# Two transformer blocks on one core: the first weight slot in halves, norms turned by a diagonal, unread passes in PE's waits, one slot of the SSD loop moved

## Chip, cores and metric

The kernel runs on one core of a Trainium2 chip. The metric is the device time of one execution in microseconds, the median of the runs shown. Everything is computed in float32 accuracy; products with weights are made of three rounded products (fp32r), as told below.

## The reference, cut to what matters

```python
# x: 256 tokens x 1024; all weights float32
# first block
h = rmsnorm(x, norm_mix_pre); proj = h @ w_in            # then three mixers, gates, branches
x = x + rmsnorm(mixed @ w_out, norm_mix_post)            # norm 1, "use 0"
h = rmsnorm(x, norm_ffn_pre)                             # norm 2, turn 1
x = x + rmsnorm((silu(h @ gate) * (h @ up)) @ down, norm_ffn_post)   # norm 3, "use 1"
# second block
h = rmsnorm_2(x, norm1_g)                                # norm 4, turn 2
# HGRN2, mLSTM and Mamba-2 SSD mixers; the SSD ends with
yz = (y_ssd + mb_d * xs) * silu(z); y_mb = rmsnorm_2(yz in 4 groups, mb_norm_g)
x = x + mixed @ w_out
u = causal_dwconv(rmsnorm_2(x, norm2_g) @ w_up, ...)     # norm 5, turn 3
x = x + (silu(u_g) * u_v) @ w_down
return rmsnorm_2(x, final_g)                             # norm 6, no turn
def rmsnorm(x, g): return x * rsqrt(mean(x * x) + EPS) * g
```

The norm in front of the first projection is norm 0, turn 0.

## The kernel before, in words

**Layout.** The residual X holds 256 tokens as two halves h of 128 partitions with 1024 channels in two chunks c of 512. Projections want channels on partitions, so each normed input is turned: X is scaled by 1/rms, transposed on PE in 16 blocks of 128x128 and multiplied by the gain while it is read out of PSUM into XH (rounded, ACT) and XL (the rest, DVE).

**The weight stream.** 170 slots of 128x2048 words (1 MB) are loaded by SP in order into a ring of three (`raw`). For each, ACT makes `whi` (rounded, line 274, `split_hi`) and DVE `wlo` (the rest, line 281, `split_lo`), and PE does 48 products of 256 columns (line 286: XH with whi, XL with whi, XH with wlo). SP loads slot p into the place of p - 3 once `lo_ready` of that is there. `Stream.go(1)` on PE is one such slot; on ACT and DVE it is the split of slot p + 2 and then the evacuation of slot p - 1. The order of `go` and the other work on each engine is written out by hand. The first pair behind each turn (`first_pair`, line 300) takes its products in the order in which XH and XL become ready.

**The norms.** `norm_act` squares the four chunks on ACT (line 576), with the sums in a column, and takes the root (line 583); `norm_bias` (589) and the reciprocal (594) are DVE's. `scale_dve` (625) then multiplies X by the reciprocal, 512 columns at a time, and `turn_pe` (651) transposes with the identity. `post_dve` (603, 610) multiplies the output of `w_out` or `down` by its gain and adds it, scaled, to X. `add_dve` (617) only adds. ACT needs the table that has the root; `load_sqrt` (667) runs a small root at a chosen place, so that the table is loaded there. In norm 3 this stands behind the first square; for norm 6 there is none, and the load comes with the first root.

**The start.** SP issues X in two halves, the identity, the columns of gains (PC), three slots and the small tables. DVE waits for the identity and for PC ahead of its first norm. PE waits for the identity ahead of `turn_pe`.

**The SSD stage.** `ssd_pe`, `ssd_act` and `ssd_dve` go over 16 heads. For each head PE spreads a row over the partitions (1213) and does one slot; ACT makes relu and exp of it (1421, 1424) and one `go`; DVE multiplies (1459) and does one `go`. Each second head's product is added up (1383, 1466). Behind the loop DVE gates the result with z (1470), ACT squares it (1428), PE sums the squares over channels (1389), and the next slot follows.

**The tail.** Behind the last `down` slot, DVE adds four chunks (617) and scales and gains each in one operation (1913); SP stores four chunks (261).

Of the kernel before, what the change touches and what calls it, by code (L numbers as in the profile page):

```python
# [29 lines left out]
F32 = mybir.dt.float32  # L30
# [7 lines left out]
D = 1024  # L38
# [134 lines left out]
def program(nc, ctx, stream, xt, cols, consts, masks, g1w, g2w, poolw, rows_w, rows, gains, out):  # L173
# [61 lines left out]
    def _(sp):  # L235
# [23 lines left out]
        for n, (h, c) in enumerate(CHUNKS):  # L259
            sp.wait_ge(S("result_ready"), n + 1)  # L260
            sp.dma_start(out[:, h, c * 512:c * 512 + 512], scaled(h, c)).then_inc(S("result_stored"), 16)
# [43 lines left out]
    def pair_matmuls(pe, p, slot, form, rewrite=None):  # L305

        pe.wait_ge(lo_ready, p + 1)
# [231 lines left out]
    def acc(h, c):  # L539

        return bank(3 + h - 2 * c)
# [22 lines left out]
    def norm_act(act, n, use=None, loaded=False, updated=None):  # L564

        order = CHUNKS if use is None else (ORDER_OUT if use in (0, 2) else ORDER_DOWN)
        for i, (h, c) in enumerate(order):
# [10 lines left out]
            if i == 0 and use in (1, 3):  # L578
                load_sqrt(act)
# [15 lines left out]

    def post_dve(dve, n, use):

        gain = words(POST_GAIN[n], 0, D)
        dve.wait_ge(S("gain_loaded"), 16 * (n // 2 + 1))
        written = {}  # L600
        for i, (h, c) in enumerate(ORDER_OUT if use in (0, 2) else ORDER_DOWN):
            dve.wait_ge(S("norm_partial"), 4 * n + i + 1)
            written[h, c] = mark(dve, dve.tensor_tensor(scaled(h, c), acc(h, c), gain[:, c * 512:c * 512 + 512], ALU.mult))
            if c == 0:
                norm_bias(dve, n, h, i)
                continue
            norm_scale(dve, n, h)
            settled(dve, written[h, 1])
            for k in range(2):
                dve.scalar_tensor_tensor(chunk(h, k), scaled(h, k), stat(n, 8 + h), chunk(h, k), ALU.mult, ALU.add)\  # L610
                   .then_inc(S("x_updated"), 1)

    def add_dve(dve, use):

        for i, (h, c) in enumerate(CHUNKS):
            wait_acc(dve, use, (ORDER_OUT if use in (0, 2) else ORDER_DOWN).index((h, c)))
            dve.tensor_tensor(chunk(h, c), chunk(h, c), acc(h, c), ALU.add).then_inc(S("x_updated"), 1)

    def scale_dve(dve, n):

        for h in range(2):
            norm_bias(dve, n, h, 2 * h)
            norm_scale(dve, n, h)
            for c in range(2):
                dve.tensor_scalar(scaled(h, c), chunk(h, c), stat(n, 8 + h), None, ALU.mult).then_inc(S("x_scaled"), 1)
# [726 lines left out]
    def ssd_pe(pe, st):  # L1352
# [16 lines left out]
        for h in range(17):  # L1369
            if h < 16:  # L1370
# [3 lines left out]
                st.go(1)  # L1374
            if h and h % 2 == 0:
# [9 lines left out]
                i.then_inc(S("mb_o"), 1)  # L1385
        for t in range(8):
# [10 lines left out]
    def ssd_act(act, st):  # L1397
# [16 lines left out]
        for h in range(16):  # L1414
# [10 lines left out]
            st.go(1)  # L1425
# [14 lines left out]
    def ssd_dve(dve, st):  # L1440
# [10 lines left out]
        for h in range(17):  # L1451
            if h < 16:
# [8 lines left out]
                st.go(1)  # L1461
# [261 lines left out]
    def _(act):  # L1723
# [4 lines left out]
        split_hi(act, 0, 0, 0)  # L1728
# [79 lines left out]
        norm_act(act, 5, updated=8)  # L1808
# [4 lines left out]
        norm_act(act, 6, updated=12)  # L1813

    @block.vector
    def _(dve):
# [7 lines left out]
        dve.wait_ge(S("consts_loaded"), 16)  # L1824
        dve.wait_ge(S("cols_loaded"), 16)
        for h in range(2):
            dve.wait_ge(S(f"x_loaded{h}"), 16)
        scale_dve(dve, 0)
        split_lo(dve, 0, 0)
# [71 lines left out]
        add_dve(dve, 2)  # L1901
        scale_dve(dve, 5)
# [3 lines left out]
        add_dve(dve, 3)  # L1906
        dve.wait_ge(S("gain_loaded"), 48)
        gain = words(POST_GAIN[6], 0, D)
        for h in range(2):
            norm_bias(dve, 6, h, 2 * h)  # L1910
            norm_scale(dve, 6, h)
            for c in range(2):
                dve.scalar_tensor_tensor(scaled(h, c), chunk(h, c), stat(6, 8 + h), gain[:, c * 512:c * 512 + 512], ALU.mult, ALU.mult)\
                   .then_inc(S("result_ready"), 1)
# [118 lines left out]
```

## Time and profile before

| | |
|---|---|
| median of 3 runs | 1173.26 us (1172.8 to 1174.63) |
| the profiled execution | 1174.35 us, span 1172.6 us |
| busy: PE / DVE / ACT | 94% / 64% / 52% of the span |
| mean granted clock of PE | 0.977 |
| weights and inputs read | 182.17 MB, 156 GB/s over the span |

PE is matmuls, PEld its weight loads beside them, DVE, ACT and SP the other engines. Times in the rows are microseconds from the span's start. A row of the timeline has start, duration, engine, line, operation, what it writes and reads, how many were merged, and in square brackets the idle time of the engine before it and what ended it. The granted clock is a share of full speed.

### The profile page before, as it was taken

To read this page: it belongs to the slowest core of one execution; us is meant where nothing else is said; L and a number is where in the kernel's file an instruction comes from. 1 tells how busy PE (TensorE), PEld (TensorE's weight loads), DVE (VectorE), ACT (ScalarE), POOL (GpSimd) and SP (SyncE) were. 2 spreads that over 40 slices of the span, in tenths; PEclk is the share of its full clock that TensorE was granted. 3 is DMA by queue.
4 is the path that set the end of the run, shared out by engine and by line. 5 is a ranking of instruction groups with operands and counts; after the bars stand their busy time and mean duration, and the time that the engine had idled before them with its cause. 6 is when DMAs were issued, how large, how long until landed. Compare 5 with 4: busy or idle time off the path is not lost. (4 is left out here: it accounts for less than half of the span.)

```text
span 1172.6 us, 22496 instructions
## 1 busy us (share of the span) xinstructions
PE 1106.7 (94%) x9384; PEld 1048.6 (89%) x9384; DVE 753.7 (64%) x980; ACT 606.0 (52%) x784; POOL 0.2 (0%) x4
## 2 busy tenths in 40 slices
PE   6999999989999998999897899899998998999997
PEld 5999999978999997899897899889997988999996
DVE  6355566677555555688687535964646767777775
ACT  5464546345444345578564534646454446554554
POOL 0000000000000000000000000000000000000000
PEclk9999999999999998999898899999999999999999
DMA  7433434454555542344333323343443454555540
GB/s 288 177 109 110 180 144 149 176 207 162 183 185 195 190 179 108 144 157 168 109 144 110 108 108 144 144 144 134 155 176 112 181 188 155 189 204 179 179 179 37
DMA packets 26967, 184.39 MB, mean 157 GB/s; under 512 B 3064, under 2 KB 3592, under 8 KB 5128
## 3 DMA queue, kind: packets, MB, share of 16 engines
q1 hardware_dynamic: 26312, 181.38, 42.7%
q10 hardware_dynamic: 576, 1.85, 0.5%
q8 instruction: 63, 1.03, 0.3%
q14 instruction: 16, 0.13, 0.0%
HBM read 182.17 MB, written 1.05 MB: 156 GB/s over the span
## 5 line engine op out<-in xcount | busy, mean ns | idle before, releaser
L281 DVE TENSOR_TENSOR wlo<-raw,whi 128x2048 fp32r<-128x2048 f32 x170 | 388.7, 2290 | 226.9 <-ACT whi L274 222.6
L286 PE MATMUL pp<-XH,whi 128*128 128x256 f32 x1696 | 486.4, 287 | 5.7 <-DVE P L404 3.2
L286 PE MATMUL pp<-XL,whi 128*128 128x256 f32 x1696 | 481.6, 284 | 0.0
L286 PE MATMUL pp<-XH,wlo 128*128 128x256 f32 x1696 | 481.4, 284 | 0.0
L274 ACT ACTIVATE whi<-raw 128x2048 fp32r<-128x2048 f32 x170 | 323.7, 1910 | 60.3 <-PE pp L286 42.5
L286 PEld LDWEIGHTS pp<-XH,whi 128*128 128x128 f32 x1696 | 327.1, 193 | 11.7 <-DVE P L404 3.8
L286 PEld LDWEIGHTS pp<-XL,whi 128*128 128x128 f32 x1696 | 327.2, 193 | 0.8
L286 PEld LDWEIGHTS pp<-XH,wlo 128*128 128x128 f32 x1696 | 327.0, 193 | 0.0
L286 PE MATMUL pp<-Y,whi 128*128 128x256 f32 x480 | 87.2, 283 | 0.4 <-DVE HF L419 0.2
L1588 ACT ACTIVATE Y<-P 128x256 fp32r<-128x256 f32 x44 | 18.4, 418 | 132.7 <-DVE P L1621 132.7
L286 PEld LDWEIGHTS pp<-Y,whi 128*128 128x128 f32 x480 | 75.1, 192 | 0.9 <-DVE HF L419 0.4
L1534 PE MATMUL pm<-whi,Y 128*128 128x512 f32 x176 | 68.8, 391 | 0.2 <-DVE Y L1611 0.2
L1535 PE MATMUL pm<-wlo,Y 128*128 128x512 f32 x176 | 68.7, 390 | 0.0
L1536 PE MATMUL pm<-whi,Y 128*128 128x512 f32 x176 | 68.5, 389 | 0.0
L286 PE MATMUL pp<-Y,wlo 128*128 128x256 f32 x240 | 67.9, 283 | 0.0
L286 PE MATMUL pp<-whi,XH 128*128 128x256 f32 x192 | 55.3, 288 | 0.0
L286 PE MATMUL pp<-wlo,XH 128*128 128x256 f32 x192 | 54.3, 283 | 0.0
L286 PE MATMUL pp<-whi,XL 128*128 128x256 f32 x192 | 54.3, 283 | 0.0
L1605 DVE SCALAR_TENSOR_TENSOR P<-pp,PC,P 128x255 f32<-128x255 f32 (+1 forms) x88 | 36.4, 476 | 25.4 <-ACT P L1579 25.4
L286 PEld LDWEIGHTS pp<-Y,wlo 128*128 128x128 f32 x240 | 46.0, 192 | 0.0
L1536 PEld LDWEIGHTS pm<-whi,Y 128*128 128x128 f32 x176 | 33.0, 188 | 7.0
L1534 PEld LDWEIGHTS pm<-whi,Y 128*128 128x128 f32 x176 | 33.1, 188 | 6.9 <-DVE Y L1611 0.6
(296 smaller groups left out, 1291.9 us busy)
## 6 DMA issues: line engine op xcount, KB each, us to landing
raw<-stream SPq DMA_DIRECT2D x170, 1024.0 KB, 4.8
P<-gains ACTq DMA_DIRECT2D x3, 512.0 KB, 3.3
X<-xt SPq DMA_DIRECT2D x2, 512.0 KB, 4.6
out<-P SPq DMA_DIRECT2D x4, 256.0 KB, 2.0
C<-consts SPq DMA_DIRECT2D x1, 345.5 KB, 11.5
P<-rows_w ACTq DMA_DIRECT2D x1, 272.0 KB, 2.8
U<-poolw SPq DMA_DIRECT2D x1, 256.0 KB, 10.4
PC<-cols SPq DMA_DIRECT2D x1, 177.0 KB, 5.3
```

Source lines behind the costliest of these rows:

```text
L274: act.activation(whi[:, slot, :], raw[:, slot, :], ACT.Copy).then_inc(hi_ready, 1)
L281: dve.tensor_tensor(wlo[:, slot, :], raw[:, slot, :], whi[:, slot, :].bitcast(F32), ALU.subtract).then_inc(lo_ready, 1)
L286: done = pe.matmul(dst, a, b, start=first and n == 0, stop=last and n == 2, **kw)
L1534: pe.matmul(dst, Y[:, y, t], whi[:, slot, at:at + 512], start=first, stop=False, skip_group_check=True)
L1535: pe.matmul(dst, Y[:, y, t], wlo[:, slot, at:at + 512], start=False, stop=False, skip_group_check=True)
L1536: return pe.matmul(dst, Y[:, 4 + y, t], whi[:, slot, at:at + 512], start=False, stop=last, skip_group_check=True)
L1588: act.activation(Y[:, par, :], pr, ACT.Copy).then_inc(S("hidden_hi"), 1)
L1605: i = dve.scalar_tensor_tensor(c[:, lag:], src[:, 0:256 - lag], fcol("ffn_conv_w", g + (44 * k + off)), c[:, lag:], ALU.mult, ALU.add)
```

## The change

- **First slot in halves.** Slot 0 is loaded as two halves, the first ahead of the columns PC. `first_hi` and `first_lo` split each half as it comes; DVE's wait for PC moves behind them.
- **Diagonal.** `diagonal_scale` multiplies the 128x128 identity by 1/rms, and PE multiplies X, as it stands, with this diagonal (a plain f32 product) in place of the transposes.
- **Unread passes.** `turn_pe` first runs 18, 27, 27 or 8 matmuls into bank 0, which nothing reads, then waits for the scale.
- **Norms.** `load_sqrt` stands at the head of norms 3 and 6; DVE's order in `post_dve` is new for use 1; norm 5 takes its squares in the order in which the chunks are finished.
- **Last norm.** The gain is multiplied before the root, the scale after it, half of it on ACT; stores wait for their own chunk.
- **SSD.** The slot (and ACT's and DVE's `go`) of head 0 is left out and stands behind the loop: on PE ahead of the sums of squares, on ACT ahead of the squares, on DVE behind the gate.

```diff
         sp.dma_start(C[:, 0:CLEVEL], consts[:, 0:CLEVEL]).then_inc(S("consts_loaded"), 16)
+        sp.dma_start(raw[:, 0, 0:PW // 2], stream[0, :, 0:PW // 2]).then_inc(S("first_arrived"), 16)
         sp.dma_start(PC[:, :], cols).then_inc(S("cols_loaded"), 16)
-        for p in range(RING):
+        sp.dma_start(raw[:, 0, PW // 2:], stream[0, :, PW // 2:]).then_inc(arrived[0], 16)
+        for p in range(1, RING):
             load(p, p)
...
+    def first_hi(act):
+        act.wait_ge(S("first_arrived"), 16)
+        act.activation(whi[:, 0, 0:PW // 2], raw[:, 0, 0:PW // 2], ACT.Copy).then_inc(S("first_hi_ready"), 1)
+        act.wait_ge(arrived[0], 16)
+        act.activation(whi[:, 0, PW // 2:], raw[:, 0, PW // 2:], ACT.Copy).then_inc(hi_ready, 1)
+    def first_lo(dve):
+        for ready, done, at in ((S("first_hi_ready"), S("first_lo_ready"), slice(0, PW // 2)), (hi_ready, lo_ready, slice(PW // 2, PW))):
+            dve.wait_ge(ready, 1)
+            dve.tensor_tensor(wlo[:, 0, at], raw[:, 0, at], whi[:, 0, at].bitcast(F32), ALU.subtract).then_inc(done, 1)
...
+                if rewrite == 0 and need == "x_hi" and k % 4 == 0:
+                    pe.wait_ge(lo_ready if k else S("first_lo_ready"), 1)
...
+        if n in (3, 6):
+            load_sqrt(act)
         for i, (h, c) in enumerate(order):
...
-            if i == 0 and use in (1, 3):
-                load_sqrt(act)
...
+            first = [post_gain(dve, n, use, 0, 0)]
+            norm_bias(dve, n, 0, 0)
+            first.append(post_gain(dve, n, use, 0, 1))
+            norm_scale(dve, n, 0)
+            post_add(dve, n, 0, first)
+            norm_bias(dve, n, 1, 2)
+            second = [post_gain(dve, n, use, 1, 0), post_gain(dve, n, use, 1, 1)]
+        norm_scale(dve, n, 1)
+        post_add(dve, n, 1, second)
...
+    def diagonal_scale(dve, n, h):
+        norm_scale(dve, n, h)
+        dve.tensor_scalar(scale_of(h), ident, stat(n, 8 + h), None, ALU.mult).then_inc(S("x_scaled"), 1)
...
+    def idle_passes(pe, tile, width, n):
+        for _ in range(n):
+            pe.matmul(bank(0)[:, 0:width], tile[:, 0:128], tile[:, 0:width], start=True, stop=True)
+    IDLE_PASSES = {0: (RF, 384, 18), 1: (CR, 256, 27), 2: (CR, 256, 27), 3: (CR, 256, 8)}
     def turn_pe(pe, r):
+        if r == 0:
+            pe.wait_ge(S("scalars_set"), 5)
+        elif r == 1:
+            pe.wait_ge(S("masks_rounded"), 2)
+        idle_passes(pe, *IDLE_PASSES[r])
         for h in range(2):
+            pe.wait_ge(S("x_scaled"), 2 * r + h + 1)
             for j in range(KT):
-                if j % 4 == 0:
-                    pe.wait_ge(S("x_scaled"), 4 * r + 2 * h + j // 4 + 1)
-                i = pe.transpose(turned(j)[:, h * 128:h * 128 + 128], scaled(h, j // 4)[:, (j % 4) * 128:(j % 4) * 128 + 128], ident)
+                i = pe.matmul(turned(j)[:, h * 128:h * 128 + 128], X[:, h, j * 128:j * 128 + 128], scale_of(h), start=True, stop=True)
...
                 spread_row(pe, bank(h % 2), h, True).then_inc(S("mb_decay"), 1)
-                st.go(1)
+                st.go(1 if h else 0)
...
+        st.go(1)
         for t in range(8):
             if t % 4 == 0:
                 pe.wait_ge(S("mb_squares"), t // 4 + 1)
...
             act.activation(e, e, ACT.Exp, scale=-1.0).then_inc(S("mb_exp"), 1)
-            st.go(1)
+            st.go(1 if h else 0)
+        st.go(1)
         for b in range(2):
             act.wait_ge(S("mb_u"), b + 1)
...
             dve.tensor_tensor(x, x, P[:, XZ + 4 * b:XZ + 4 * b + 4, :], ALU.mult).then_inc(S("mb_u"), 1)
+        st.go(1)
         dve.wait_ge(S("mb_rms"), 1)
...
-        norm_act(act, 5, updated=8)
+        norm_act(act, 5, updated=8, order=ORDER_OUT)
...
         norm_act(act, 6, updated=12)
+        last_scale_act(act, 0, 1)
+        last_scale_act(act, 1, 1)
...
-        add_dve(dve, 2)
-        scale_dve(dve, 5)
+        add_dve(dve, 2, 0, 0)
+        add_dve(dve, 2, 1, 0)
+        norm_bias(dve, 5, 0, 0)
+        norm_bias(dve, 5, 1, 1)
+        add_dve(dve, 2, 0, 1)
+        add_dve(dve, 2, 1, 1)
+        diagonal_scale(dve, 5, 0)
+        diagonal_scale(dve, 5, 1)
...
+        add_dve(dve, 3, 0, 0)
+        last_gain(dve, 0, 0)
+        add_dve(dve, 3, 0, 1)
+        norm_bias(dve, 6, 0, 0)
+        last_gain(dve, 0, 1)
+        add_dve(dve, 3, 1, 0)
+        dve.wait_ge(S("norm_rms"), 13)
+        dve.reciprocal(stat(6, 8), stat(6, 6)).then_inc(S("last_scales"), 1)
+        dve.wait_ge(S("last_scales"), 1)
+        last_scale_dve(dve, 0, 0)
+        add_dve(dve, 3, 1, 1)
+        norm_bias(dve, 6, 1, 2)
+        last_gain(dve, 1, 0)
+        last_gain(dve, 1, 1)
+        dve.wait_ge(S("norm_rms"), 14)
+        dve.reciprocal(stat(6, 9), stat(6, 7)).then_inc(S("last_scales"), 1)
+        dve.wait_ge(S("last_scales"), 2)
+        last_scale_dve(dve, 1, 0)
```

## Rows read from the trace of the kernel before

**Rows 1.** The page's busy times, share of the span and instructions.
```profile
PE 1106.7 (94%) x9384; PEld 1048.6 (89%) x9384; DVE 753.7 (64%) x980; ACT 606.0 (52%) x784; POOL 0.2 (0%) x4
```
**Rows 2.** Timeline around turns 1, 2 and 3.
```profile
266.22 3.63 PE L651 MATMUL pm<-C,P 128*128 128x128 f32 x16 [4.19 <-DVE P L625]
275.86 0.39 PE L286 MATMUL pp<-XH,whi 128*128 128x256 f32 x1 [0.23 <-DVE wlo L281]
454.61 1.28 ACT L667 ACT_TABLE_LOAD   x1
462.54 0.88 DVE L625 TENSOR_SCALAR P<-X,SC 128x512 f32<-128x512 f32 x2
463.08 3.68 PE L651 MATMUL pm<-C,P 128*128 128x128 f32 x16 [5.12 <-DVE P L625]
973.42 1.10 PE L651 MATMUL pm<-C,P 128*128 128x128 f32 x8 [1.95 <-DVE P L625]
```
**Rows 3.** Busy times by window; the last three columns are clock, DMA, GB/s.
```profile
466.50:467.50 1.00, 1.00 (x7) 1.00 (x6) 1.00 (x3) 1.00 (x4) 0.00 (x0) 0.50 0.00 0
972.00:974.00 2.00, 0.58 (x5) 0.59 (x6) 1.36 (x6) 1.61 (x6) 0.00 (x0) 1.00 0.00 0
```
**Rows 4.** Timeline of the start, and the identity's time from issue to landing.
```profile
1.66 0.42 SPq L242 DMA_DIRECT2D C<-consts  x1
...
C<-consts SPq DMA_DIRECT2D x1, 64.0 KB, 5.1
...
7.55 0.15 DVE L589 TENSOR_SCALAR SC<-SC 128x1 f32<-128x1 f32 x1 [4.17 <-DMA PC<-cols]
11.77 3.01 ACT L660 ACTIVATE XH<-pm,PC 128x256 fp32r<-128x256 f32 x8
14.24 0.58 PE L300 MATMUL pp<-XH,whi 128*128 128x256 f32 x1 [1.63 <-DVE wlo L281]
16.32 0.41 PE L300 MATMUL pp<-XH,wlo 128*128 128x256 f32 x1
16.54 0.41 PE L300 MATMUL pp<-XH,whi 128*128 128x256 f32 x1
19.42 2.08 PE L300 MATMUL pp<-XL,whi 128*128 128x256 f32 x16
21.34 0.28 PE L286 MATMUL pp<-XH,whi 128*128 128x256 f32 x1
```
**Rows 5.** Timeline of the SSD loop's first head and of its end.
```profile
793.13 0.73 ACT L1421 ACTIVATE P<-pm,SC 128x256 f32<-128x256 f32 x2 [0.53 <-PE pm L1213]
794.33 1.90 ACT L274 ACTIVATE whi<-raw 128x2048 fp32r<-128x2048 f32 x1
898.82 2.19 ACT L1428 ACTIVATE P<-P 128x1024 f32<-128x1024 f32 x2 [5.46 <-DVE P L1470]
899.93 5.30 PE L1389 MATMUL pm<-P,C 128*4 128x256 f32 x16 [3.15 <-ACT P L1428]
```
**Rows 6.** Timeline of the tail, and the stores' time from issue to landing.
```profile
1162.61 0.69 DVE L617 TENSOR_TENSOR X<-X,pm 128x512 f32<-128x512 f32 x1 [0.67 <-PE pm L1536]
1163.97 0.69 DVE L617 TENSOR_TENSOR X<-X,pm 128x512 f32<-128x512 f32 x1 [0.67 <-PE pm L1536]
1164.80 1.28 ACT L583 ACT_TABLE_LOAD   x1 [2.10 <-DVE SC L589]
DMA to landing us min/median/max: 2.0/2.0/2.0
```
**Rows 7.** Timeline of f32 products and transposes, at half and at full clock.
```profile
786.14 0.63 PE L1359 MATMUL pm<-P 128*128 128x128 f32 x2
786.56 1.06 PE L1358 MATMUL pm<-P 128*128 128x256 f32 x2
789.26 0.38 PE L1359 MATMUL pm<-P 128*128 128x128 f32 x2
789.48 1.04 PE L1365 MATMUL pm<-C,P 128*128 128x128 f32 x8
```

More of the change, by code:

```diff
@@ L562, in stat, with norm_act @@
         return SC[:, at:at + 1]
-    def norm_act(act, n, use=None, loaded=False, updated=None):
-        order = CHUNKS if use is None else (ORDER_OUT if use in (0, 2) else ORDER_DOWN)
+    def norm_act(act, n, use=None, loaded=False, updated=None, order=None):
+        order = order or (CHUNKS if use is None else (ORDER_OUT if use in (0, 2) else ORDER_DOWN))
+        if n in (3, 6):
+            load_sqrt(act)
         for i, (h, c) in enumerate(order):
@@ L594, in norm_scale, with post_gain, post_add @@
         link(dve, dve.reciprocal(stat(n, 8 + h), stat(n, 6 + h)))
+    def post_gain(dve, n, use, h, c):
+        dve.wait_ge(S("norm_partial"), 4 * n + (ORDER_OUT if use in (0, 2) else ORDER_DOWN).index((h, c)) + 1)
+        gain = words(POST_GAIN[n], 0, D)[:, c * 512:c * 512 + 512]
+        return mark(dve, dve.tensor_tensor(scaled(h, c), acc(h, c), gain, ALU.mult))
+    def post_add(dve, n, h, gained):
+        for c in range(2):
+            settled(dve, gained[c])
+            dve.scalar_tensor_tensor(chunk(h, c), scaled(h, c), stat(n, 8 + h), chunk(h, c), ALU.mult, ALU.add)\
+               .then_inc(S("x_updated"), 1)
@@ L596, in post_dve @@
     def post_dve(dve, n, use):
-        gain = words(POST_GAIN[n], 0, D)
         dve.wait_ge(S("gain_loaded"), 16 * (n // 2 + 1))
[L600 to L617, printed above, removed]
+        if use == 0:
+            first = [post_gain(dve, n, use, 0, 0)]
+            norm_bias(dve, n, 0, 0)
+            second = [post_gain(dve, n, use, 1, 0)]
+            norm_bias(dve, n, 1, 1)
+            first.append(post_gain(dve, n, use, 0, 1))
+            norm_scale(dve, n, 0)
+            post_add(dve, n, 0, first)
+            second.append(post_gain(dve, n, use, 1, 1))
+        else:
+            first = [post_gain(dve, n, use, 0, 0)]
+            norm_bias(dve, n, 0, 0)
+            first.append(post_gain(dve, n, use, 0, 1))
+            norm_scale(dve, n, 0)
+            post_add(dve, n, 0, first)
+            norm_bias(dve, n, 1, 2)
+            second = [post_gain(dve, n, use, 1, 0), post_gain(dve, n, use, 1, 1)]
@@ L619, in scale_dve, with add_dve @@
+        norm_scale(dve, n, 1)
+        post_add(dve, n, 1, second)
+    def add_dve(dve, use, h, c):
+        wait_acc(dve, use, (ORDER_OUT if use in (0, 2) else ORDER_DOWN).index((h, c)))
+        dve.tensor_tensor(chunk(h, c), chunk(h, c), acc(h, c), ALU.add).then_inc(S("x_updated"), 1)
+    def diagonal_scale(dve, n, h):
+        norm_scale(dve, n, h)
+        dve.tensor_scalar(scale_of(h), ident, stat(n, 8 + h), None, ALU.mult).then_inc(S("x_scaled"), 1)
     def scale_dve(dve, n):
@@ L622, in scale_dve, with last_gain, last_scale_dve, last_scale_act @@
             norm_bias(dve, n, h, 2 * h)
-            norm_scale(dve, n, h)
-            for c in range(2):
-                dve.tensor_scalar(scaled(h, c), chunk(h, c), stat(n, 8 + h), None, ALU.mult).then_inc(S("x_scaled"), 1)
+            diagonal_scale(dve, n, h)
+    def last_gain(dve, h, c):
+        dve.wait_ge(S("x_updated"), 12 + 2 * h + c + 1)
+        dve.tensor_tensor(scaled(h, c), chunk(h, c), words(POST_GAIN[6], c * 512, 512), ALU.mult).then_inc(S("last_gained"), 1)
+    def last_scale_dve(dve, h, c):
+        dve.wait_ge(S("last_gained"), 2 * h + c + 1)
+        dve.tensor_scalar(scaled(h, c), scaled(h, c), stat(6, 8 + h), None, ALU.mult).then_inc(S(f"result_ready{h}{c}"), 1)
+    def last_scale_act(act, h, c):
+        act.wait_ge(S("last_gained"), 2 * h + c + 1)
+        act.wait_ge(S("last_scales"), h + 1)
+        act.activation(scaled(h, c), scaled(h, c), ACT.Copy, scale=stat(6, 8 + h)).then_inc(S(f"result_ready{h}{c}"), 1)
+    def scale_of(h):
+        return P[:, 44, h * 128:h * 128 + 128]
     def turn_lo(dve, n, gain):
@@ L1460, in ssd_dve @@
                                              cb_words(h // 4)[:, at], ALU.mult, ALU.mult).then_inc(S("mb_w"), 1)
-                st.go(1)
+                st.go(1 if h else 0)
             if h and h % 2 == 0:
@@ L1824, in _ @@
         dve.wait_ge(S("consts_loaded"), 16)
+        scale_dve(dve, 0)
+        first_lo(dve)
         dve.wait_ge(S("cols_loaded"), 16)
[L1826 to L1829, printed above, removed]
         turn_lo(dve, 0, "norm_mix_pre")
```

17 lines of the change are left out of this document (5 added, 12 removed).

## The prediction

> **What bounds the kernel now.** I read the page's busy shares first, then the waits of PE, then the timeline around each place where PE stands still, then the granted clock there. PE is busy 94% of the span and no other engine is near [rows 1], so nearly everything that the change can bring lies in PE's standstills, in stretches where PE runs at half clock, and behind its last matmul. The diff touches six such places: the start, three later turns of a norm, the sums of squares of the SSD stage, and the tail.
>
> What the reader is to see in the rows: before the turns PE stands still for 4.19, 5.12 and 1.95 us; the 16 transposes then take 3.63 and 3.68 us at half clock (0.23 each), while in the last turn, where PE has stood for less, 8 take 1.10 (0.12 to 0.14 each) [rows 2]. The granted clock is 0.50, the level of 1.2 GHz, until behind turn 2, and 1.00, 2.4 GHz, in turn 3 [rows 3]. At the start the products tell of the lower level: 256-column ones follow each other in 0.21 us, and once it is up 16 of them take 2.08, 0.12 each and the last one's tail [rows 4]. The sums of squares are reached after a wait of 3.15 us, and their 8 products (16 records) then take 5.30 [rows 5]. In the tail, 1.28 us of table load stand between PE's last matmul and the first square root [rows 6].
>
> **Diagonal for transpose.** The turn itself becomes a plain f32 product of 128 columns. The nearest rows are products of that form in the SSD stage, two records each: one at half clock lasts from 786.14 to 786.56, 0.42 us; one at full clock from 789.26 to 789.48, 0.22. Transposes follow there, 8 in 1.04 [rows 7]. So 16 diagonals cost 3.5 us warm and 6.7 cold, against 1.9 to 2.2 and 3.65 for transposes: the diagonal pays only with a clock that is up. On DVE, one multiply of a 128x128 tile takes the place of a 512-wide one before PE can begin: bounds 0.15 (the 128x1 multiply, [rows 4]) and 0.44 (half of the pair's 0.88, [rows 2]); I take 0.20, since 128 columns are nearer to the short end, a gain of 0.24 per half.
>
> **The unread passes.** They stand in PE's queue ahead of the wait for the scale. Turns 1 and 2 get 27 of 256 columns, at 0.12 each 3.2 us: they end inside the standstills of 4.19 and 5.12 and leave 0.7 and some 1.2 us of rest. Turn 3 gets 8, 1.0 us of its 1.95. A standstill of 1.95 did not lower the clock in turn 3 [rows 2, 3], so I take the clock as held in all three. What is queued behind the passes is only the turn.
>
> **Turn 1** (before 266.22 to 269.85): the start comes 0.27 earlier and the 16 products take 3.5 instead of 3.63; the second half, whose end sets XH, the next splits and the second pair, comes out 0.35 earlier. The new order of DVE's post-norm for this use is the old one. **-0.35.**
>
> **Turn 2**: besides the 0.24, the table load leaves the place between the first two squares. It ends at 455.9 [rows 2], and with the small root behind it the second square starts at 456.1. Chunks end 1.36 apart (1162.61 and 1163.97 in [rows 6], where the same matmuls run), the first near 453.85, the second near 455.2: the square may start 0.9 earlier. DVE then is the queue: four multiplies and four adds of about 0.7 each. It starts them 0.8 earlier, and with the second half's two multiplies now both behind the first half's adds it hands 0.5 on (bounds 0 and 0.9). Turn starts at about 462.35 instead of 463.08, and its second half 0.8 earlier. The first pair no longer begins at half clock [rows 3], but the second pair stands behind the split that follows XH on ACT (as in turn 1, at 275.86 in [rows 2]), so this adds nothing to the 0.8. **-0.8.**
>
> **Turn 3** was warm, so here the diagonals are dearer by 8 x 0.10 = 0.8 per half. Against it, squares are taken in the order in which chunks are finished, so the first half's root and scale no longer wait for the last add: PE starts at about 972.6 instead of 973.42, and runs both halves without a stop; the second begins at 974.3 instead of about 975.0. Its first two products take 0.44 instead of 0.24. **-0.45** (bounds +0.3, if the products eat it, and -0.8).
>
> **SSD.** PE's slot of head 0 moves behind the last head's product. The chain that PE waited for (DVE's product, the gate, ACT's squares from 898.82 to 901.0) ends 4.2 us after PE stopped at 896.8 [rows 5]; a slot is 48 x 0.12 = 5.75 us, so it covers all of it, and the wait of 3.15 goes. PE does not rest, so the sums run warm: a 256-column f32 product is twice the 0.22 of [rows 7], 8 x 0.44 = 3.5 instead of 5.30, -1.8. On ACT and DVE the moved slot holds a split and an evacuation. ACT's stand ahead of its squares, but it does them while it would wait for the gate; DVE's stand behind the gate. What is late next is the loop's beginning: with no slot in head 0, PE reaches its second in-loop slot after heads 0, 1 and 2 have been spread, while ACT must do relu and exp of heads 0 and 1 before the split. For one head they took from 793.13 to 794.33, where the split began [rows 5], and a wait for exp lies between; with two it begins at 795.7; with 1.9 and 2.3 for the two halves of it the weights are ready at 800.0, and PE would want them at 799.2: +0.9 once, later heads have PE's old rhythm. **-3.15 - 1.8 + 0.9 = -4.05** (bounds: -5 if the head start costs nothing, -1 below).
>
> **The last norm and the stores.** PE ends at 1163.93, and the add that it releases starts at 1163.97. The old chain from there: add, bias, table load 1.28, root, two scales, bias, root, two scales, store; the span ends 8.7 us after PE [rows 6]. New: the table is loaded while ACT idles; gains are multiplied before the root; the first half's root is taken before PE ends. DVE after PE's end: scale of the first chunk until 1164.4, last add to 1165.05, bias, two gains (0.69 each like the add of [rows 6], overlapping a little) to 1166.6, reciprocal 1166.8, one scale to 1167.4. ACT: last square 1165.1 to 1165.9, root, two scales, the last from 1166.9 to 1167.5. SP issues the last two stores behind each other (its issue was 0.34 each), the last at 1167.8, lands 2.0 later: 1170.1 or 1170.2. **-2.4** (bounds -1.3, the table load alone, and -2.8).
>
> **The start.** The wait of PE for the identity stays ahead of the turn, and so of the passes. The identity is issued at 1.66 and lands 5.1 later, 6.8 [rows 4]. So 18 passes of 384 columns start at 6.85, not with the kernel. At half clock each takes 384/256 x 0.21 = 0.32 (5.8 for all), at full half of it. PE's run from 14.24 was cold still at 16.54, after 2.3 us [rows 4], that from 463.08 until at least 467.5, after 4.4 [rows 2, 3]. Taking 3.4, the middle: 10.6 cold passes and 7.4 warm, end 11.45. The scale is there by about 7.9 (DVE no longer waits for the columns until 7.55), and by 11.45 so is everything else: the passes have become the bound. Diagonals end at 15.0. XH begins at 13.85 rather than 11.77 [rows 4], and with 3.1 for XH, 1.9 and 2.3 for the next split, second pair's weights stand at about 21.1. It began at 21.34. What the halves of the first slot gain (its lo part at 12.1 instead of 14.2, a warm first pair) is used up there: **-0.1 to +1.2, taken +0.1.** If the passes cost nothing, the gain would be 1.7.
>
> The Trainium skill (TensorE: Matmul & The Clock Gate, section "What's actually happening") has the moment at which the clock rises vary from run to run, since the chip's look at activity does not start with the kernel. By that rule the start would come out anywhere between -0.1 and +1.2. The trace agrees so far as its runs of PE stay cold for different lengths, over 2.3 us here and over 4.4 there.
>
> **Sum**: -0.35 - 0.8 - 0.45 - 4.05 - 2.4 + 0.1 = -7.95. The profiled execution took 1174.35 (span 1172.6), 1.1 above the median of 1173.26; from it the sum gives 1166.4, from the median 1165.3. I give 1165.3.
>
> **Rivals.**
> A. *The clock falls in spite of the passes* (they end 0.7 to 1.2 us before the turn). For: the standstills of turns 1 and 2 did lower it, and the passes leave part of them. Against: 1.95 in turn 3 did not. Each cold turn costs 16 x 0.20 = 3.2 more; this decides from three of four turns on (9.6 > 7.95); all four give 1178.1. The slower side.
> B. *The SSD wait only moves*: the loop now begins a head short, and if each early head waits for its split, the 3.15 comes back there, leaving some 1 us. For: one head's relu, exp and split (1.2 and 1.9) and DVE's 0.8 and 2.3 behind them fill over 5.5 of a slot's 5.75 us. Against: PE caught no wait there in later heads. 1168.4.
> C. *The start loses*: the clock rises only after all 18 passes, first diagonals cold. Passes end at 12.6, chain +1.2 to +2: 1167.
> D. *The start gains*: passes warm at once, end at 9.7, chain -1.7: 1163.5. Against: no run of PE out of a cold clock was warm within 2.3 us.
> E. *The gain of the SSD slot and the norms is absorbed behind* (weights not split in time). Against: the second pair of turn 1 already stands right behind its split, with 0.23 of wait (275.86, and so in turn 3), and the shifts above are counted along that split. 1171, little chance.
>
> **How the numbers follow.** Forecast 0.62 (own range 1163.8 to 1167), A 0.04, B 0.12, C 0.11, D 0.07, E 0.04. The range to hold it 8 times in 10 reaches into B, C and D: 1162.8 to 1168.8. A measurement here tells 0.2%, 2.35 us. Below 1170.9: forecast, B, C, D and some of E; leaving room for what no row shows, faster 0.88, same 0.08, slower 0.04.
>
> **What would show it.** Granted clock 1.00 from the end of the output pairs through the first pair in turns 1 to 3, L651's successor at 0.22 per product; no wait of PE at the sums of squares and 3.5 us for them; a new wait of about 0.9 at the second slot of the SSD loop; no table load behind PE's last matmul and 6.2 us from there to the end; passes from 6.8 to about 11.5 at the start, second pair near 21.3. The prediction is wrong if the diagonals take over 0.3 each, if the wait at the sums stays, or if the second pair starts outside 20 to 23.

## The result, and the profile after

The changed kernel takes 1164.22 us (median of 5, 1163.53 to 1167.93); the kernel before, on the same chip, 1173.21 (5, 1172.8 to 1174.63). The ratio is 0.9931, with a 95% interval of 0.9913 to 0.9949: faster by 9.0 us, where 7.95 was forecast (1165.3, range 1162.8 to 1168.8). The profiled execution of the changed kernel took 1163.53, its span is 1161.4, so it is 11.2 shorter than the span of before, 1172.6. How far 11.2 and 9.0 can be explained by the terms of the sum is the question of this part. In what follows PE is cold at the lower level of its clock and warm at the full one. A cold or a warm turn is one that runs so.

The page's busy times of the changed kernel, to be set against [rows 1]:

```profile
PE 1114.2 (96%) x9528; PEld 1058.9 (91%) x9528; DVE 749.8 (65%) x975; ACT 607.8 (52%) x788; POOL 0.2 (0%) x4
```

PE is busy for longer, 7.5 us, although the whole got shorter: the passes and the second record of each diagonal count as work, and the standstills went.

The start in the timeline of the changed kernel, PE's turn and what feeds it (start, duration, engine and line, tile), against [rows 4]:

```profile
6.20 6.13 PE L707 MATMUL pm<-RF 128*128 128x384 f32 x18 [6.20 <-DMA C<-consts]
...
6.96 0.28 DVE L658 TENSOR_SCALAR P<-C,SC 128x128 f32<-128x128 f32 x1
...
8.54 1.06 ACT L288 ACTIVATE whi<-raw 128x1024 fp32r<-128x1024 f32 x1 [0.26 <-DMA raw<-stream]
...
9.63 1.22 DVE L296 TENSOR_TENSOR wlo<-raw,whi 128x1024 fp32r<-128x1024 f32 x1 [0.83 <-ACT whi L288]
...
12.13 3.83 PE L721 MATMUL pm<-P,X 128*128 128x128 f32 x32
14.72 3.02 ACT L730 ACTIVATE XH<-pm,PC 128x256 fp32r<-128x256 f32 x8 [3.36 <-PE pm L721]
...
15.71 0.36 PE L317 MATMUL pp<-XH,whi 128*128 128x256 f32 x1
...
21.93 0.39 PE L301 MATMUL pp<-XH,whi 128*128 128x256 f32 x1 [0.22 <-DVE wlo L283]
```

The first scale is there at 7.24 and the first half of the first slot's columns is split by 10.9, yet the diagonals begin at 12.13: ahead of them stand 18 passes at some 0.33 us each. The passes begin 0.65 sooner than the forecast's 6.85, since the identity lands 4.5 us after its issue (5.1 before). The second pair starts at 21.93, 0.59 later than the 21.34 of before.

Turns 1, 2 and 3, against [rows 2]; the row of the table load belongs to turn 2:

```profile
262.61 3.40 PE L707 MATMUL pm<-CR 128*128 128x256 f32 x27
...
266.77 3.84 PE L721 MATMUL pm<-P,X 128*128 128x128 f32 x32 [0.76 <-DVE P L658]
...
453.06 1.28 ACT L737 ACT_TABLE_LOAD   x1
...
455.93 0.60 ACT L596 ACTIVATE P<-pm 128x512 f32<-128x512 f32 x1 [0.62 <-PE pm L1609]
...
458.46 3.40 PE L707 MATMUL pm<-CR 128*128 128x256 f32 x27
462.67 3.84 PE L721 MATMUL pm<-P,X 128*128 128x128 f32 x32 [0.82 <-DVE P L658]
...
962.84 1.12 PE L707 MATMUL pm<-CR 128*128 128x256 f32 x8
...
964.18 3.84 PE L721 MATMUL pm<-P,X 128*128 128x128 f32 x32 [0.22 <-DVE P L658]
```

All three sets of 32 records take 3.84, 0.12 for a record: the clock is up. The windows say the same, and they show where else the kernel now runs at full or at half clock, against [rows 3]. First the changed kernel, then the kernel before (start and end of the window, its length, busy times of PE, weight loads, DVE, ACT and POOL; then granted clock, DMA share, GB/s):

```profile
251.00:255.00 4.00, 4.00 (x12) 3.15 (x11) 3.29 (x2) 0.78 (x3) 0.00 (x0) 0.57 0.89 346
461.00:463.00 2.00, 1.18 (x11) 0.98 (x10) 1.31 (x5) 1.20 (x4) 0.00 (x0) 1.00 0.00 0
466.50:467.50 1.00, 1.00 (x11) 1.00 (x10) 1.00 (x4) 1.00 (x4) 0.00 (x0) 1.00 0.06 16
785.00:789.00 4.00, 3.00 (x23) 2.44 (x22) 1.27 (x4) 3.04 (x7) 0.00 (x0) 1.00 0.00 0
...
665.00:673.00 8.00, 7.44 (x59) 7.36 (x60) 6.77 (x9) 4.04 (x6) 0.00 (x0) 1.00 0.43 141
```

```profile
785.00:789.00 4.00, 3.85 (x13) 3.40 (x14) 2.88 (x5) 2.87 (x4) 0.00 (x0) 0.57 0.00 0
665.00:673.00 8.00, 6.45 (x30) 6.29 (x31) 5.84 (x6) 5.03 (x6) 0.00 (x0) 0.57 0.34 125
```

Two falls of the clock, around 669 and 787, are gone at places that no line of the diff touches, and one has come, around 253. The changed kernel runs some 4 us ahead there, so a window does not hold the same work in both, but from 641 to 1159 its granted clock is 1.00 throughout. A third is gone around 108 (granted clock 0.66 from 105 to 110 before, 1.00 after). It and the new one nearly cancel: from the second pair at the start to turn 1 the kernel before takes 240.69 us, the changed one 240.84.

The SSD loop's head and its sums, against [rows 5]:

```profile
788.41 0.61 PE L1283 MATMUL pm<-RF,CR 128*128 128x384 f32 x2 [0.69 <-ACT P L1484]
...
795.63 0.35 PE L301 MATMUL pp<-XH,whi 128*128 128x256 f32 x1 [0.68 <-DVE wlo L283]
...
889.30 2.20 ACT L1500 ACTIVATE P<-P 128x1024 f32<-128x1024 f32 x2 [3.66 <-DVE P L1542]
...
893.13 3.62 PE L1460 MATMUL pm<-P,C 128*4 128x256 f32 x16
```

The sums have no wait and take 3.62 instead of 5.30. The squares are ready at 891.5 and PE comes at 893.1. The new wait at the second slot is there, 0.68.

The tail, against [rows 6]:

```profile
1149.15 1.28 ACT L737 ACT_TABLE_LOAD   x1
...
1155.18 3.77 SPq L263 DMA_DIRECT2D out<-P  x4
1155.23 0.69 DVE L653 TENSOR_TENSOR X<-X,pm 128x512 f32<-128x512 f32 x1
...
1156.90 1.32 ACT L680 ACTIVATE P<-P,SC 128x512 f32<-128x512 f32 x2
...
1157.29 0.48 DVE L674 TENSOR_SCALAR P<-P,SC 128x512 f32<-128x512 f32 x1
```

PE's last matmul ends at 1155.19, 6.2 ahead of the end of the span; in the kernel before it was 8.7.

**Where the 11.2 us lie.** The same anchors (the end of PE's last matmul ahead of a turn and of its passes, the second pair behind it, the first f32 product of the SSD stage, the first product behind its sums, PE's end) cut both spans into the same stages:

| stage | before | after | difference | forecast |
|---|---|---|---|---|
| start to second pair | 21.34 | 21.93 | +0.59 | +0.1 |
| turn 1 | 13.83 | 13.73 | -0.10 | -0.35 |
| turn 2 | 14.85 | 13.79 | -1.06 | -0.8 |
| turn 3 | 11.20 | 10.91 | -0.29 | -0.45 |
| SSD stage | 120.01 | 115.18 | -4.83 | -4.05 |
| tail | 8.65 | 6.23 | -2.42 | -2.4 |
| second pair of turn 2 to SSD stage | 312.33 | 309.09 | -3.24 | 0 |
| all other stretches | | | +0.19 | 0 |

The six named places give -8.11, near the -7.95. The rest, -3.05, is one fall of the clock that the new profile does not have where the old one had it (665 to 673). I do not count it as a gain: runs 3 and 4 below differ from the changed kernel in its first 8 us alone, and take 313.8 in that stretch. Executions scatter with such falls, the five of the changed kernel had spans of 1161.4, 1164.6, 1162.0, 1165.9 and 1162.2 at mean granted clocks of 0.989, 0.985, 0.987, 0.983 and 0.987, and the profiled one, the first, is the fastest of them.

### The profile page after: what moved, and what is told of

Read it like the earlier page. It is cut to its first block and busy times, and to the rows that moved or that the text cites. A ratio compares the mean times of both kernels' runs of the same rounds, so it can differ in the third digit from the quotient of the medians.

```text
span 1161.4 us, 22790 instructions
## 1 busy us (share of the span) xinstructions
PE 1114.2 (96%) x9528; PEld 1058.9 (91%) x9528; DVE 749.8 (65%) x975; ACT 607.8 (52%) x788; POOL 0.2 (0%) x4
## 5 line engine op out<-in xcount | busy, mean ns | idle before, releaser
L301 PEld LDWEIGHTS pp<-XH,whi 128*128 128x128 f32 x1696 | 326.1, 192 | 13.8 <-issue 4.1
```

## The experiments

The theory was the sum as forecast, part by part. Each run takes one part out or puts one part in alone, and the stage table tells what it is worth where it stands. Ratios are against runs of the kernel before on the same chip.

**1. Without the SSD slot.** The changed kernel, with the slot back in head 0:

```
-                st.go(1 if h else 0)
+                st.go(1)
...
-        st.go(1)
```

(the same on ACT and DVE).

> The changed kernel with the SSD stage's slot put back into head 0 and taken from the place ahead of the sums of squares, all else changed. Theory (the slot covers the chain from the last product to the squares and keeps the clock up for the sums): the wait of about 3.15 us at the sums is back, they take 5.3 us or at least more than 3.6 if the clock falls, the new wait of 0.7 to 0.9 us at the second slot of the loop is gone; 3.5 to 4.5 us slower than the changed kernel, about 1168.3. Rival (the wait only moved to the loop's head): at most 1 us slower, about 1165.

1167.15 us (1165.05 to 1173.08, 7), ratio 0.9954 (0.9935 to 0.9973). The wait and the slow sums are back together in the timeline:

```profile
894.61 5.30 PE L1459 MATMUL pm<-P,C 128*4 128x256 f32 x16 [3.15 <-ACT P L1498]
```

The SSD stage takes 119.43 instead of 115.18: this part is worth 4.25. The medians show 2.9 of it; the seven executions spread over 8 us.

**2. Without the passes of turns 1 to 3.**

```
-    IDLE_PASSES = {0: (RF, 384, 18), 1: (CR, 256, 27), 2: (CR, 256, 27), 3: (CR, 256, 8)}
+    IDLE_PASSES = {0: (RF, 384, 18), 1: (CR, 256, 0), 2: (CR, 256, 0), 3: (CR, 256, 0)}
```

> The changed kernel without the unread passes of turns 1, 2 and 3 (the 18 at the start stay). Theory (the passes hold the clock, and the diagonal pays only with it): the clock falls in turns 1 and 2, where PE then rests 4 to 5 us; their 16 products take 6.8 instead of 3.5 us; +3.2 in each, +6.4 in all, about 1170.6; turn 3 keeps its clock and its time. Rival (the clock would have stayed up in a rest that is now shorter, or its fall is luck of alignment): no more than 3 us slower.

1166.97 us (1165.04 to 1170.95, 6), ratio 0.9949 (0.9932 to 0.9965). The diagonals of turns 1 and 2 in the timeline:

```profile
267.45 5.44 PE L721 MATMUL pm<-P,X 128*128 128x128 f32 x32 [4.08 <-DVE P L658]
...
464.66 6.26 PE L721 MATMUL pm<-P,X 128*128 128x128 f32 x32 [4.05 <-DVE P L658]
```

Turn 1 is 1.40 longer, turn 2 2.14, turn 3 not at all (10.91). So the passes do hold the clock where PE would stand for 4 us, and the 8 passes of turn 3 hold nothing: without them PE stands for 1.18 and the clock stays up. A cold turn costs less than the 3.2 of rival A, since the clock rises inside the diagonals: 32 records at half clock would last 6.7.

**3. PE's wait for the identity taken away from the passes, and 4. no passes at the start.** The passes read a tile that DVE writes, so they need not stand behind that wait; the diagonals have their own, through the scale.

```
-        pe.wait_ge(S("consts_loaded"), 16)
```
```
-    IDLE_PASSES = {0: (RF, 384, 18), 1: (CR, 256, 27), 2: (CR, 256, 27), 3: (CR, 256, 8)}
+    IDLE_PASSES = {0: (RF, 384, 0), 1: (CR, 256, 27), 2: (CR, 256, 27), 3: (CR, 256, 8)}
```

> The changed kernel with PE's wait for the identity taken from in front of turn 0 (the wait for the scale, which is made from the identity, covers it). The 18 passes then start at about 1.9 us instead of 6.2. Theory (the passes at the start are the bound there since they start late): products start at 7.8 or so instead of 12.1, second pair at 18.8 instead of 21.9, -3 us, about 1161. Rival (the first slot's arrival and its split set the second pair anyway): under 1 us.

> The changed kernel without the 18 passes at the start, all else the same. Theory (the passes cost more than the clock they bring): 16 products at half clock from 7.2 us, 6.8 us, end 14.2 instead of 15.7; XH begins at 11.7 instead of 14.7; second pair near 20.0 instead of 21.9, -1.9 us, about 1162.3. Rival (a cold clock costs more than the passes: products at 0.42 and a cold first pair): second pair at 23 or later, +1 us or more.

Run 3: 1163.57 us (1159.91 to 1164.93, 5), 0.9904 (0.9885 to 0.9922). Run 4: 1160.83 (1157.77 to 1166.34, 6), 0.9893 (0.9873 to 0.9914). PE's rows at the start, run 3 and then run 4:

```profile
1.84 5.38 PE L707 MATMUL pm<-RF 128*128 128x384 f32 x18 [1.84 <-DVE RF L1896]
...
7.39 3.84 PE L721 MATMUL pm<-P,X 128*128 128x128 f32 x32 [0.17 <-DVE P L658]
...
18.46 0.39 PE L301 MATMUL pp<-XH,whi 128*128 128x256 f32 x1 [0.31 <-DVE wlo L283]
```

```profile
7.45 5.29 PE L721 MATMUL pm<-P,X 128*128 128x128 f32 x32 [7.45 <-DVE P L658]
...
18.71 0.39 PE L301 MATMUL pp<-XH,whi 128*128 128x256 f32 x1 [0.22 <-DVE wlo L283]
```

The second pair comes 3.47 and 3.22 earlier than in the changed kernel. Run early, the passes make the diagonals 1.45 faster, but of that only 0.25 reaches the second pair; where the diff puts them they cost 3.2 in this profile. Run 3's median shows only 0.7 of its 3.5 us: three of its five executions, the profiled one among them, lie at 1163.6 to 1164.9 with a clock of 0.985, two at 1159.9 and 1160.4 with 0.989. Its profile and run 4's have the fall of the clock ahead of the SSD stage that the changed kernel's lacks. Run 4 came out 1.3 us better at the second pair than its theory, since the clock rises inside its diagonals (5.29 instead of 6.8).

**5. The SSD slot alone,** in the kernel before:

```
-                st.go(1)
+                st.go(1 if h else 0)
...
+        st.go(1)
```

> The kernel before with the moved SSD slot alone. Theory: no wait of PE at the sums of squares, which take 3.6 us instead of 5.3; a new wait of 0.7 to 0.9 us at the second slot of the loop; from the start of the SSD stage's first product to the end of the sums 4.0 to 4.8 us less than before. In the median some 4 us less, as far as the scatter of the clock (2 to 4 us between executions) lets it be seen. Rival (wait only moves): under 1 us within the stage.

1169.22 us (1166.99 to 1171.02, 6), ratio 0.996 (0.9947 to 0.9973): 4.1 faster by the medians. Its SSD stage takes 115.80, -4.21 against before. It still has the fall of the clock at its start:

```profile
785.00:789.00 4.00, 3.24 (x10) 2.81 (x11) 2.88 (x3) 2.75 (x4) 0.00 (x0) 0.60 0.00 0
665.00:673.00 8.00, 5.96 (x25) 5.81 (x26) 5.85 (x6) 5.51 (x7) 0.00 (x0) 0.58 0.29 99
```

So -4.2 belongs to the slot, and the other 0.6 of the -4.83 to the fall around 787. Runs 3 and 4, which have the changed kernel's SSD stage together with that fall, agree: 115.74 and 115.73 against 115.18.

**6. ACT and DVE one head later.** In the changed kernel ACT and DVE do their `go` of head 0 again and leave out that of head 1, so that the split that PE waits for no longer stands behind relu and exp of two heads. PE's order stays (the same edit on DVE):

```
-            st.go(1 if h else 0)
+            st.go(0 if h == 1 else 1)
```

> The changed kernel, with ACT and DVE doing the first moved turn of the loop in head 0 again and leaving out that of head 1 (PE as changed). Theory (the new wait at the second slot is ACT's relu and exp of two heads ahead of the split): the wait of 0.7 to 0.9 us at the second slot of the loop is gone, the stage is that much shorter, and nothing later changes. Rival (the wait comes from DVE's multiplies or PE's own order): it stays.

1164.37 us (1161.4 to 1168.97, 6), ratio 0.993 (0.9907 to 0.9953). The wait at the second slot is gone, the SSD stage takes 114.25, 0.93 less. The median does not show it: six executions of this kernel spread over 7.6 us. It is shown by the stage alone.

**7. The table load alone,** taken out of the tail of the kernel before, into ACT's idle time ahead of the last norm's squares:

```
+        if n == 6:
+            load_sqrt(act)
```

> The kernel before with one edit: the table with the root is loaded at the head of the last norm, while ACT idles, nothing else. Theory (table load is 1.28 of the tail's 2.4 us): from PE's last matmul to the end of the span 7.4 us instead of 8.67. Rival (the load hides behind DVE's four adds, which end when the bias is made): 8.3 or more.

1172.46 us (1170.12 to 1174.31, 12), ratio 0.9993 (0.9984 to 1.0001). The tail takes 7.36 instead of 8.65, -1.29, and nothing else moves (turn 2 14.89, SSD 120.01). The median alone would not show it: its interval reaches over 1. The other 1.13 of the tail's 2.42 is left for the gain ahead of the root and the earlier first half; no run takes these apart. The Trainium skill (ScalarE: Activation LUTs, section "What ACT_TABLE_LOAD costs") puts a load at about 1283 ns, and adds a drain of about 1380 ns at every switch. The load agrees with the 1.28 of [rows 6]; the drain does not show here, as taking the load away brought 1.29 and not 2.7. In that tail ACT had been idle for 2.10 ahead of the load, but in turn 2 of the kernel before ACT works until 454.59, loads from 454.61 to 455.89 [rows 2] and goes on at 455.90.

**8. Transposes instead of diagonals.** The changed kernel with everything but the diagonal: DVE scales 512 columns, PE transposes them.

```
-        dve.tensor_scalar(scale_of(h), ident, stat(n, 8 + h), None, ALU.mult)
+        for c in range(2):
+            dve.tensor_scalar(scaled(h, c), chunk(h, c), stat(n, 8 + h), None, ALU.mult)
...
-                i = pe.matmul(turned(j)[...], X[:, h, j * 128:j * 128 + 128], scale_of(h), start=True, stop=True)
+                i = pe.transpose(turned(j)[...], scaled(h, j // 4)[...], ident)
```

> The changed kernel with the passes, but with transposes of the scaled X in place of the diagonals in all four turns. Theory (with the clock up a transpose takes 0.12 and a diagonal 0.22; the diagonal gains 0.2 us on DVE in front and loses 0.2 on the first two products of the second half that XH waits for): second pairs of turns 1 to 3 within 0.3 us of those of the changed kernel, so the diagonal itself brings nothing and the passes carry the gain. Rival (the diagonal is what makes the turn shorter): second pairs 0.5 us or more later in each turn.

1160.31 us (1158.83 to 1162.57, 5), ratio 0.9894 (0.988 to 0.9908), 3.9 faster than the changed kernel by the medians, of which the stages show 2.6. The theory, that the diagonal brings nothing, was too kind to it. Turn 1 in the timeline:

```profile
259.54 3.40 PE L708 MATMUL pm<-CR 128*128 128x256 f32 x27
263.90 1.09 PE L723 MATMUL pm<-C,P 128*128 128x128 f32 x8 [0.96 <-DVE P L659]
265.47 1.09 PE L723 MATMUL pm<-C,P 128*128 128x128 f32 x8 [0.47 <-DVE P L659]
```

PE starts 0.20 later than with diagonals (0.96 of rest instead of 0.76), and then 16 transposes take 2.66 with their gap where 16 diagonals took 3.84. The turns are shorter by 0.28, 0.29 and 0.64, the start by 1.37. The diagonal is a loss in all four places as the change has them. At the start that is so for as long as the 18 passes stand in front: from their end to the second pair it is 8.56 us with transposes and 9.70 to 9.80 in the four profiles with diagonals. With an early start it turns round, as runs 9 and 10 show.

What is left is the gain of the turns without the diagonal. In turn 1 it is that of the passes, for run 12 (the passes alone) has 13.44 and this run 13.46. In turn 3 the passes bring nothing (run 2), which leaves the new order of the squares: 10.27 instead of 11.20. In turn 2 the passes, DVE's order and the table load come together.

**12. The passes alone,** in the kernel before, with its transposes and its order of DVE, ahead of the turn:

```
+        if r:
+            if r == 1:
+                pe.wait_ge(S("masks_rounded"), 2)
+            idle_passes(pe, CR, 256, (0, 27, 27, 8)[r])
```

> The kernel before with the unread passes of turns 1, 2 and 3 alone, nothing at the start. Theory (the passes hold the clock): granted clock 1.00 through turns 1 and 2, transposes at 0.12; second pairs 0.4 to 0.6 us earlier relative to PE's end in each of the two, nothing in turn 3; some 1 us in all, 1172.2. Rival (passes do nothing for transposes, which wait for DVE anyway): under 0.3 us in all.

1170.67 us (1169.27 to 1174.14, 9), ratio 0.9974 (0.9964 to 0.9984). Turn 1 is 0.39 shorter, turn 3 unchanged (11.20). Turn 2 takes 14.91 against 14.85, for the clock fell inside it. PE's rows, and the windows of the same stretch:

```profile
457.38 3.39 PE L648 MATMUL pm<-CR 128*128 128x256 f32 x27
462.66 1.09 PE L660 MATMUL pm<-C,P 128*128 128x128 f32 x8 [1.88 <-DVE P L625]
464.22 1.97 PE L660 MATMUL pm<-C,P 128*128 128x128 f32 x8 [0.47 <-DVE P L625]
```

```profile
461.00:463.00 2.00, 0.34 (x3) 0.35 (x4) 1.54 (x6) 1.41 (x5) 0.00 (x0) 1.00 0.00 0
463.00:465.00 2.00, 1.53 (x11) 1.29 (x10) 1.11 (x4) 0.45 (x4) 0.00 (x0) 0.77 0.00 0
465.00:467.00 2.00, 2.00 (x11) 1.89 (x10) 1.18 (x3) 2.00 (x6) 0.00 (x0) 0.50 0.00 0
```

Here the table load still stands between the squares, the turn comes later, and PE rests for 1.88 behind the passes. In the changed kernel it rests for 0.82 and the clock holds. So in this execution the passes alone brought nothing at turn 2. That is one execution, the slowest of the nine; the median is 2.5 us below the kernel before, more than the 0.4 that its stages show, and in the faster ones turn 2 may have stayed warm. No run has the earlier turn with transposes and without passes, so how the 1.35 us of turn 2 in run 8 is shared between the two is not shown.

**9, 10 and 11. What the runs point to.** Run 9 joins runs 8, 6 and 3; run 10 is run 9 without the 18 passes (run 4's edit); run 11 is run 9 with the first slot loaded and split whole:

```
-        sp.dma_start(raw[:, 0, 0:PW // 2], stream[0, :, 0:PW // 2]).then_inc(S("first_arrived"), 16)
...
-        first_hi(act)
+        split_hi(act, 0, 0, 0)
...
-        first_lo(dve)
+        split_lo(dve, 0, 0)
```

> Transposes in place of the diagonals, the 18 passes of the start from 1.9 us on (PE's wait for the identity taken from in front of turn 0), and ACT's and DVE's first turn of the SSD loop in head 0; the rest as changed. Theory (each part adds to the kernel with transposes): start's second pair near 18.5 us instead of 20.6, -2; loop head -0.9; about 1157.5. Rival (gains of the start are lost behind it, to the arrival of the next slots): about 1159.5.

> The kernel of the run before this one without the 18 passes at the start. Theory (the first slot's arrival and ACT's two halves of its split set XH at about 11.3 us, whatever PE's clock): second pair within 0.4 us of the one with the passes, 18.5 to 18.9; the same time within the scatter. Rival (the first pair at half clock takes 6.8 instead of 3.8 us and becomes the bound): second pair 1 us or more later.

> The kernel with transposes and the early 18 passes, with the first slot loaded and split whole as before the change. Theory (with PE early, the first slot's arrival at about 10 us and its split on ACT ahead of XH are the bound; halves save half a split there): XH 0.8 to 0.9 us later, second pair near 19.4; the halves are worth 0.9 us. Rival (the columns or the scale are the bound): under 0.3 us.

| run | us (range, executions) | ratio (interval) | second pair | turns 1, 2, 3 | SSD |
|---|---|---|---|---|---|
| 9 | 1159.09 (1156.73 to 1162.42, 5) | 0.988 (0.9862 to 0.9897) | 19.65 | 13.44, 13.50, 10.27 | 114.24 |
| 10 | 1157.84 (1156.94 to 1158.61, 4) | 0.9864 (0.9849 to 0.9878) | 19.66 | 13.44, 13.50, 10.26 | 114.24 |
| 11 | 1161.07 (1159.94 to 1164.45, 5) | 0.9895 (0.9881 to 0.9908) | 21.70 | 13.44, 13.50, 10.26 | 114.80 |

The 18 passes bring nothing even early: with them the transposes are warm, but PE then stands for 2.12 and the first pair begins to run at half clock 0.6 us later. For the same reason run 9 missed its theory (second pair near 18.5, 1157.5 us). PE's rows of run 9:

```profile
1.83 5.34 PE L708 MATMUL pm<-RF 128*128 128x384 f32 x18 [1.83 <-DVE RF L1898]
...
12.30 0.39 PE L317 MATMUL pp<-XH,whi 128*128 128x256 f32 x1 [2.12 <-ACT XH L732]
...
13.07 0.42 PE L317 MATMUL pp<-XH,wlo 128*128 128x256 f32 x1
13.29 0.42 PE L317 MATMUL pp<-XH,whi 128*128 128x256 f32 x1
```

With diagonals the same early start did better. Run 3 has run 9's start with diagonals and reaches the second pair at 18.46, not 19.65; run 4 stands so against run 10, 18.71 against 19.66. The first pairs start within 0.2 us of each other (12.14 and 12.30, 12.50 and 12.44). But with diagonals the first pair is warm throughout, 0.12 from product to product, and with transposes its products are 0.21 apart until 16.3 in run 9 and 15.4 in run 10. Each is one profile. Transposes in turns 1 to 3 with diagonals at the start were not run; by these rows I estimate about 1 us more.

The halves of the first slot are worth 2.05, more than twice what run 11's theory had: the first pair starts at 12.30 with them, at 14.39 without (run 11), and the second pair moves by as much. The theory counted ACT's half split alone. In run 11 the whole slot also lands later (ACT begins it at 10.01, not 8.72), and DVE's whole split of 2.29, not XH, is what PE waits for.

Run 10 has the lowest median, though its interval overlaps run 9's: 15.3 us below the kernel before and 6.4 below the change as made. Of these 6.4 the stages show 4.4 (start 2.27, turns 0.29, 0.29 and 0.65, SSD 0.94).

## Why the prediction held, and where its steps were off

**SSD, -4.05; measured -4.2** (run 5; run 1 gives 4.25 in the other direction). Each part came as worked out: the wait of 3.15 went, the sums are 1.68 shorter (I took 1.8), the new wait is 0.68 (0.9). Run 6 shows that it is caused as told, by the split behind two heads' relu and exp, since moving that split removes it. Rival B, the wait that comes back, is out: the loop has the one wait of 0.68 and no other above 0.2.

**Tail, -2.4; measured -2.42,** of which 1.29 is the table load (run 7). PE's last matmul to the end is 6.2, as forecast.

**Turn 2, -0.8; measured -1.06.** The second square starts 0.9 earlier, as worked out, and the diagonals start 1.06 earlier instead of 0.73; then 0.17 of that is eaten by the diagonals until the first pair, and 0.17 won back until the second. That the passes are what holds the clock there is shown by run 2. The reason that the prediction gave, that a standstill of 1.95 had not lowered it, was not safe: run 12 lost it behind 1.88. What was left behind the passes was shorter, 0.76 and 0.82, and turns 1 and 2 took 13.7 and 13.8 in all five profiles that have diagonals and passes there.

**Turn 1, -0.35; measured -0.10. Turn 3, -0.45; measured -0.29.** The term that was mis-sized is the diagonal, on both engines. DVE's multiply takes 0.29, I took 0.20, "nearer to the short end", and the bounds were 0.15 and 0.44; and the 32 records take 3.84 from first start to last end, where 3.5 was put against the 3.63 of before, which has its last record's tail in it. In turn 3 the diagonals' start came 0.78 earlier (0.8 forecast) and up to the first pair their length took back 0.57. The step "the diagonal pays only with a clock that is up" was too kind: run 8 has the clock up, and there the diagonal is 0.3 dearer in turns 1 and 2 and 0.64 in turn 3.

**The start, +0.1; measured +0.59 in the profile.** The mechanism was right: the passes start with the identity and are the bound (run 4: 3.2 us). Its size hung on when the clock rises. I let it rise after 3.4 us and had the passes end at 11.45; in the profile 18 passes last from 6.20 to 12.1, 0.33 each, all at half clock, and only their start 0.65 sooner than forecast kept the error small. Four profiles of this very start (the changed kernel, runs 1, 2 and 6) have the second pair at 21.93, 21.41, 21.99 and 20.77, +0.65 to -0.57 against before. Up to the diagonals the passes took 5.93, 5.57, 5.92 and 4.89, and from there to the second pair it was 9.70 to 9.80 each time: the scatter of the start is that of the passes. So +0.1 is inside what the executions do, and that it came near is in part luck. Rival C's condition, all 18 passes cold, was met in the first and third of them, but not its price of 1.2 to 2, for the diagonals were warm; rival D's, all warm, in none. What I missed is the alternative: against run 4 the passes were 2.1 to 3.3 us too dear.

**Rival A** is out for the changed kernel: the granted clock is 1.00 in all three turns. Its price of 3.2 for a cold turn was too high; run 2 has 1.40 and 2.14. **Rival E** is out: each shift of a turn's second half arrives at its second pair, and behind the SSD stage nothing is lost (from the first product behind its sums to turn 3 it is 66.3 us in both kernels).

**What no term had** are the clock's falls elsewhere. The profile of the changed kernel lacks the one around 669 (3.24 us) and gained 0.6 by the lack of the one around 787. In the medians less of it is left: 9.0 less the 7.51 of the named stages without that 0.6 leaves 1.5. Whether the edits make those falls rarer, or whether it is chance, is open. The stretch from turn 2's second pair to the SSD stage took 308.5 to 309.1 in seven of the fourteen profiles and 312.1 to 313.8 in the other seven, and runs 3 and 4, which keep turns 1 to 3 as the changed kernel has them, are among the long ones. The two falls come and go together: the seven long profiles are the seven that have the one around 787 too. I tested no edit inside that stretch.

## What to carry to other kernels

Unread passes kept the clock here where they left 1 us of rest or less ahead of PE's next work (0.76 to 0.97); with 1.88 left it fell in the one profile of it. They cost nearly their full length when they stand in front of work that is ready: start them from data that is there first, and end them before the wait is over. An f32 product with a diagonal in place of a scaled transpose lets PE begin 0.2 us earlier and costs it 1.2 us for 16 blocks, clock up; in the turns 0.3 to 0.6 us of that arrived at the second pair. At the start, where the first pair can be cold, the early diagonals came out 1.0 to 1.2 us ahead of the early transposes, in two pairs of profiles. Judge an edit of 1 us by its stage in two profiles, and look first whether the clock is the same in both there: the median of a kernel whose clock falls at changing places moves by more than that.

## What the runs showed of the hardware

The time of one and the same kernel goes with its mean granted clock: the five executions of the changed kernel lie between 0.983 (span 1165.9) and 0.989 (1161.4), in order, 4.5 us apart, while the 42 of the kernel before that ran beside the experiments had 0.976 to 0.979. These spread over 4.3 us (1169.1 to 1173.4), and not in that order: 1172.6 has 0.979 and 1171.3 has 0.976.

The same standstill does not always lower the clock. It fell in run 12 behind 1.88 us of rest, 3.39 of passes ahead of it, and not in turn 3 of before, behind 1.95 [rows 2, 3]. The Trainium skill (TensorE: Matmul & The Clock Gate, section "What's actually happening") has the moment at which the clock rises depend on where the chip's free-running look at activity happens to stand. The start agrees with it, where the same 18 passes took 4.89 to 5.93 in four profiles. Taken over to a fall, it would give what these two standstills show, but no run here could set that moment.

At the start the clock's column does not tell. The windows of the first 12 us of the changed kernel have 1.00 in it, while passes of 384 columns follow each other at 0.33 us; at full clock it would be 0.18, by the 0.12 of 256 columns. There the spacing of equal products is what must be read.
